# Scores of a differential attention: both softmax components as two 64-row matmuls under one exponential

## The chip, the cores and the metric

The kernel runs on the 8 cores of one Trainium2 chip, each core taking 2 of the 16 sequences; the cores exchange nothing. The metric is device time in microseconds (us) of the slowest core. Each core has a matmul engine (PE, TensorE), a vector engine (DVE), an activation engine (ACT), a general engine (POOL) and a queue that starts transfers (SP). They run side by side, each works its own instructions strictly in the order in which they stand, and they wait for each other on semaphores.

## The reference

One block: a normalised input is projected to five parts of 512 columns (a recurrent branch, its gate, q, k, v); a gated linear recurrence and a differential attention fill 1024 mixed columns; an output projection, then a gated feed-forward part of width 3072 with a short convolution, each with a residual; a last norm. The attention is the part that matters here:

```python
    q = q.reshape(bsz, s, DIFF_HEADS, 2, DIFF_QK)      # 4 heads, 2 components, 64 wide
    k = k.reshape(bsz, s, DIFF_HEADS, 2, DIFF_QK)
    v = v.reshape(bsz, s, DIFF_HEADS, DIFF_VDIM)       # 128 wide
    ...
        logits = jnp.einsum("bqhcd,bkhcd->bhcqk", qb, k).astype(jnp.float32) * scale   # 64 ** -0.5
        logits = logits + jnp.transpose(bias, (2, 0, 1))[None, :, None]   # same bias for both components
        mask = (k_pos // CHUNK)[None, :] <= (q_pos // CHUNK)[:, None]
        p = jax.nn.softmax(logits, axis=-1)
        w = p[:, :, 0] - lam * p[:, :, 1]
        return jnp.einsum("bhqk,bkhe->bqhe", w.astype(v.dtype), v)
```

So each head has two score matrices with a contraction of 64 each, one bias for both, two softmaxes, and one value product of their weighted difference.

## The kernel before

A core works on 8 groups of 512 positions (4 groups to a sequence). Everything is kept with channels on the 128 partitions and positions along the row. Dense work is a list of units, each of which fills one of three PSUM banks: 8 matmuls of 128x512 for a projection or feed-forward unit (lines 718, 726, 734), 24 for a unit of the feed-forward's way down (line 742). Weights come through a ring of three 1 MB slabs in SBUF. A unit's result is read out by ACT or DVE, after which the bank is free.

The attention of a group runs beside the dense units of the group before it. For each head and each block of 128 keys, and for each of the two components, there is one *tile*: a score matmul (line 1004) of 128 keys by up to 512 queries, on the diagonal and just beside it a bias addition by DVE in PSUM (line 1023), an exponential by ACT from PSUM to the bf16 tile `PT` (line 1026), and up to four matmuls of 128x129 with the values (line 1038), which gather the sum of the weights in their last column. There are 640 such tiles. The scores alternate between PSUM banks 0 and 1 (a pool "S" of two); the value sums stand in banks 2 to 4; dense units use 5 to 7.

A key tile `KT` holds a head's 128 rows: 64 of component 0 above 64 of component 1. The score matmul of one component uses all 128 rows. So that the other component adds nothing, the queries are kept twice in `qz`, each time with zeros in the other half's rows. `fin_q` (lines 748 to 766) writes them from PSUM with one instruction of 64 rows for each component, and POOL zeroes `qz` once at the start (line 494).

The order of the instructions is worked out when the program is built. `Flow.run` keeps a clock for each engine with an estimated duration for each operation (`t_pe`, `t_act`, `t_dve`, `t_pool`), and takes, again and again, the operation that could start first; ties go by priority, with attention tiles first. `attention` has a pace that spreads its tiles over the dense units. A tile gets a slot of "S" before its score matmul and gives it back once its exponential is placed. What comes out is one fixed list for each engine. Where an engine's real work is later than the estimate, the engines that wait for it wait in place.

Of the kernel before, what the change touches and what calls it, by code (L numbers as in the profile page):

```python
# [16 lines left out]
G = 512  # L17
# [360 lines left out]
def build(nseq, S, pk_off, npar, st_off, nst):  # L378
# [14 lines left out]
    with ExitStack() as st:  # L393
# [9 lines left out]
        qz = T("qz", [128, 4, 2, G], BF16)  # L403
# [4 lines left out]
        PT = T("PT", [128, 3, G], BF16)  # L408
# [12 lines left out]
        banks = [st.enter_context(nc.psum_tensor("pb%d" % i, [128, 512], F32)) for i in range(8)]  # L421
# [55 lines left out]
        SB = (0, 1)  # L477
# [16 lines left out]
        op("pool", lambda e: e.memset(qz[:], 0.0), writes=b_q, dur=4.0)  # L494
# [253 lines left out]
        def fin_q(g, h, bk):  # L748
            bank = DB[bk]
            if g > 0:  # L750
                yield need(("tq", g - 1, h))
            flip[0] ^= 1
            use_act = flip[0]
            for c in range(2):
                lo, hi = c * 64, c * 64 + 64
                if use_act:
                    yield o_act(G, lambda e, c=c, lo=lo, hi=hi: e.activation(out=qz[lo:hi, h, c, :],
                                                                            in_=banks[bank][lo:hi, :], func=AF.Copy,
                                                                            scale=0.125), [b_ps[bank]], [b_q[h]])
                else:  # L760
                    yield o_dve(G, lambda e, c=c, lo=lo, hi=hi: e.tensor_scalar(out=qz[lo:hi, h, c, :],
                                                                               in0=banks[bank][lo:hi, :],
                                                                               scalar1=0.125, scalar2=None,
                                                                               op0=ALU.mult), [b_ps[bank]], [b_q[h]])
            yield put("bank", bk)
            yield mark(("q", g, h))
# [218 lines left out]
        def attention(g, pace):  # L985
            qt = g % NG
            nj = qt * 4 + 4
            base = (g // NG) * NG
            tiles = [(h, j, c) for h in range(4) for j in range(nj) for c in range(2)]
            yield need(("setup",))  # L990
            for h in range(4):
                yield need(("q", g, h))
                yield need(("k", g, h))
                yield need(("v", g, h))
            for n, (h, j, c) in enumerate(tiles):
                if pace is not None:
                    yield need(("d", pace(n / len(tiles))))
                s_ = yield get("S")
                bank = SB[s_]
                i0 = max(0, j - qt * 4)  # L1000
                N = (4 - i0) * 128
                slot = (base + j // 4) % KVS
                jj = j % 4
                yield o_pe(t_pe(N), lambda e, bank=bank, N=N, slot=slot, h=h, jj=jj, c=c, i0=i0: e.matmul(  # L1004
                    banks[bank][:, 0:N], lhsT=KT[:, slot, h, jj * 128:(jj + 1) * 128], rhs=qz[:, h, c, i0 * 128:G],
                    start=True, stop=True), [b_K[slot][h], b_q[h]], [b_ps[bank]])
                if j == nj - 1 and c == 1:
                    yield mark(("tq", g, h))
                yield go(tile(g, n, h, j, c, s_, i0, N, slot, nj, n == len(tiles) - 1), P_T)

        def tile(g, n, h, j, c, s_, i0, N, slot, nj, last_tile):
            qt = g % NG
            bank = SB[s_]
# [7 lines left out]
            if wn:  # L1021
                bias_ap = pv("biasT", h * 256 + boff, h * 256 + boff + wn)
                yield o_dve(wn, lambda e: e.tensor_tensor(out=banks[bank][:, 0:wn], in0=banks[bank][:, 0:wn],  # L1023
                                                          in1=bias_ap, op=ALU.add), [b_ps[bank], b_bias], [b_ps[bank]])
            p = yield get("PT")
            yield o_act(N, lambda e: e.activation(out=PT[:, p, 0:N], in_=banks[bank][:, 0:N], func=AF.Exp),  # L1026
                        [b_ps[bank]], [b_PT[p]], "exp")
# [3 lines left out]
            if j == 0 and c == 0 and (g, h) != (0, 0):  # L1031
                yield need(("acc", g - 1, 3) if h == 0 else ("acc", g, h - 1))

            def f(e):
                for il in range(i0, 4):
                    ab, off = (AC + c, il * 130) if il < 3 else (AC + 2, c * 130)
                    st_flag = j == 0 and (il == 0 or (il == 3 and c == 0))
                    last = e.matmul(banks[ab][:, off:off + 129], lhsT=PT[:, p, (il - i0) * 128:(il - i0 + 1) * 128],  # L1038
                                    rhs=Va[:, slot * 4 + j % 4, h, 0:129], start=st_flag, stop=(j == qt * 4 + il),
                                    skip_group_check=True)  # L1040
                return last
            wb = [b_ps[AC + c], b_ps[AC + 2]] if i0 < 3 else [b_ps[AC + 2]]
            yield o_pe(t_pe(129, 4 - i0), f, [b_PT[p], b_V[slot][j % 4]], wb)
            yield put("PT", p)
            yield mark(("pv", g, n))
            if j == nj - 1 and c == 1:
# [245 lines left out]
        fl = Flow(S_, {"bank": 3, "S": 2, "PT": 3, "ring": NRING, "x": 8, "lru": 2, "ob": 1, "st": 2, **NPOOL})  # L1292
# [68 lines left out]
```

How the kernel before makes its waits and increments, by code:

```python
            def body(e):  # L149
                for fn, waits, sem, inc in self.prog[k]:
                    for s, v in waits:
                        e.wait_ge(self.sems[s], v)
                    if fn is not None:
                        ins = fn(e)
                        ins.then_inc(self.sems[sem], inc)
```

## Time and profile before

| | |
|---|---|
| median of 3 runs | 1935.11 us (1935.06 to 1939.55) |
| the profiled execution | 1935.9 us, span of its slowest core 1934.3 us |
| spans of the 8 cores | 1915.1 to 1934.3 us |
| PE busy | 1727.8 us, 89% of the span, 9458 matmuls |
| PE weight loads | 837.0 us |
| DVE, ACT, POOL busy | 1126.3, 1074.1, 583.7 us |

A "span" is the time from the first to the last instruction of a core. Of PE's busy time it has to be known that a matmul's record is longer than the distance between two of them: a 128x512 matmul has a record of 0.38 us, while 24 of them back to back take 5.34 us. What one costs in a stream is the distance. Idle time is counted before the instruction that ended it, with the engine and line that released it.

### The profile page before, as it was taken

How to read it: one execution, taken by the hardware profiler on the slowest of the kernel's cores; microseconds unless marked ns; L12 is line 12 of the kernel's file. 1: busy time of each engine (PE TensorE's matmuls, PEld its weight loads, DVE VectorE, ACT ScalarE, POOL GpSimd, SP SyncE). 2: the span in 40 equal slices, each digit the busy share in tenths (PEclk: the TensorE clock that was granted, in tenths of full speed). 3: DMA queues.
4: the chain of work that ended last, by engine and by line, in shares of the span. 5: the costliest groups of instructions: out<-in, count | busy, mean ns of one | idle time of the engine just before them, and what ended most of it. 6: DMA issues, size and time to landing. Idle time of an engine off the chain costs nothing.

```text
span 1934.3 us, 32122 instructions; the slowest of 8 cores (1915.1 to 1934.3 us)
## 1 busy us (share of the span) xinstructions
PE 1727.8 (89%) x9458; PEld 837.0 (43%) x9458; DVE 1126.3 (58%) x2136; ACT 1074.1 (56%) x1876; POOL 583.7 (30%) x809
## 2 busy tenths in 40 slices
PE   4774799599999989999999989999999998997996
PEld 1332344244444544444444444444444554543442
DVE  6753688327773367635884388625784167623741
ACT  3463577137782478833782277625785467932631
POOL 3523455332521214303440336112530212212201
PEclk9986899799999999999999999999999999998998
DMA  8998688434434326244634453433524334342542
GB/s 266 234 184 214 201 279 280 135 130 158 147 132 168 115 88 196 105 152 138 217 121 163 148 168 142 170 126 124 197 106 158 126 115 137 115 169 98 175 135 104
DMA packets 54569, 306.44 MB, mean 158 GB/s; under 512 B 5760, under 2 KB 5888, under 8 KB 30720
## 3 DMA queue, kind: packets, MB, share of 16 engines
q1 hardware_dynamic: 51200, 298.10, 46.6%
q0 software_dynamic: 3200, 6.29, 2.6%
q8 instruction: 81, 1.33, 0.3%
q14 instruction: 88, 0.72, 0.1%
HBM read 273.96 MB, written 42.99 MB: 164 GB/s over the span
## 4 chain that ended last, share of the span: by engine, by line
PE 80%; issue 5%; DVE 5%; ACT 5%; DMA 3%; POOL 1%; SPq 0%; DVEq 0%; ACTq 0%; POOLq 0%
PE pb L718 40%; PE pb L742 17%; PE pb L734 6%; PE pb L1004 5%; PE pb L1038 5%; PE pb L726 2%; PE pb L1253 2%; DMA xp<-wa 2%; ACT aT L815 1%; PE pb L562 1%; DMA tL<-x 1%; ACT PT L1026 1%; DVE H L603 1%; POOL tN L594 1%; DVE ob L1080 1%
## 5 line engine op out<-in xcount | busy, mean ns | idle before, releaser
L718 PE MATMUL pb<-H,ring 128*128 128x512 bf16 x3784 | 883.4, 385 | 53.5 <-ACT tL L834 22.6
L718 PEld LDWEIGHTS pb<-H,ring 128*128 128x128 bf16 x3784 | 362.6, 99 | 479.0 <-issue 104.3
L1026 ACT ACTIVATE PT<-pb 128x512 bf16<-128x512 f32 (+3 forms) x640 | 316.4, 533 | 312.0 <-PE pb L1004 195.7
L594 POOL TENSOR_TENSOR tN<-tN 128x512 f32<-128x512 f32 x161 | 206.3, 1282 | 543.0 <-ACT tN L583 537.9
L742 PE MATMUL pb<-aT,ring 128*128 128x512 bf16 x1536 | 340.5, 379 | 0.9 <-DVE aT L940 0.9
L953 DVE TENSOR_TENSOR xp<-pb,xp 128x512 f32<-128x512 f32 x128 | 88.4, 691 | 352.3 <-PE pb L742 234.7
L742 PEld LDWEIGHTS pb<-aT,ring 128*128 128x128 bf16 x1536 | 148.9, 98 | 177.8 <-issue 5.4
L1004 PE MATMUL pb<-qz,KT 128*128 128x512 bf16 (+3 forms) x640 | 190.8, 349 | 28.8 <-ACT PT L1026 26.1
L1038 PE MATMUL pb<-Va,PT 128*128 128x129 bf16 x2176 | 191.2, 221 | 26.8 <-DVE tO L1074 22.0
L940 DVE TENSOR_TENSOR aT<-pb,aT 128x512 bf16<-128x512 f32 x192 | 131.0, 685 | 119.3 <-PE pb L718 102.4
L1038 PEld LDWEIGHTS pb<-Va,PT 128*128 128x128 bf16 x2176 | 153.4, 98 | 99.1 <-issue 34.0
L583 ACT ACTIVATE tN<-xp 128x512 f32<-128x512 f32 x144 | 90.2, 630 | 189.4 <-DVE xp L953 173.8
L930 DVE SCALAR_TENSOR_TENSOR tG<-tG,prm 128x512 f32<-128x512 f32 x192 | 149.9, 786 | 52.5 <-ACT tG L923 51.2
L930 DVE SCALAR_TENSOR_TENSOR aT<-tG,prm 128x512 bf16<-128x512 f32 x192 | 159.4, 834 | 11.1 <-DVE tG L930 0.6
L923 ACT ACTIVATE tG<-pb,prm 128x512 f32<-128x512 f32 x192 | 150.3, 790 | 3.5 <-DVE aT L930 3.2
L919 ACT ACTIVATE tG<-pb 128x512 f32<-128x512 f32 x192 | 116.2, 606 | 64.0 <-PE pb L1253 33.6
L926 POOL COPY fhalo<-tG 128x2 f32<-128x2 f32 x192 | 68.0, 355 | 264.5 <-ACT tG L919 252.4
L1023 DVE TENSOR_TENSOR pb<-pb,prm 128x256 f32<-128x256 f32 (+1 forms) x304 | 106.8, 376 | 61.9 <-PE pb L1004 57.3
L734 PE MATMUL pb<-mixT,ring 128*128 128x512 bf16 x512 | 122.7, 388 | 1.9 <-ACT mixT L1104 1.9
L877 ACT ACTIVATE tL<-tL 128x512 f32<-128x512 f32 x192 | 111.9, 634 | 0.7
L1004 PEld LDWEIGHTS pb<-qz,KT 128*128 128x128 bf16 x640 | 62.7, 98 | 109.9 <-issue 45.2
L603 DVE SCALAR_TENSOR_TENSOR H<-xp,prm,tN 128x512 bf16<-128x512 f32 x120 | 85.5, 774 | 40.1 <-ACT tN L575 39.2
(95 smaller groups left out, 1518.4 us busy)
## 6 DMA issues: line engine op xcount, KB each, us to landing
ring<-wa SPq DMA_DIRECT2D x128, 1024.0 KB, 4.9
ring<-wd SPq DMA_DIRECT2D x64, 768.0 KB, 4.2
xp<-wa SPq DMA_DIRECT2D x38, 1024.0 KB, 8.5
xp<-x SPq DMA_DIRECT2D x64, 512.0 KB, 8.6
wa<-ring SPq DMA_DIRECT2D x17, 1024.0 KB, 11.2
out<-xp SPq DMA_DIRECT2D x32, 512.0 KB, 6.0
wd<-wd POOLq DMA_DIRECT2D x8, 768.0 KB, 80.6
tL<-x SPq DMA_DIRECT2D x4, 512.0 KB, 18.6
```

The costliest lines, as they stand in the source:

```text
L594: yield o_(G, lambda e: e.tensor_tensor(out=tN[:, acc, :], in0=tN[:, acc, :], in1=tN[:, sq, :], op=ALU.add), [b_N[acc], b_N[sq]], [b_N[acc]])
L718: last = e.matmul(banks[bank][:], lhsT=rv(r)[:, kk * 512 + c * 128:kk * 512 + (c + 1) * 128], rhs=hd[0][:, kk, :], start=(kk == 0), stop=( ...
L734: last = e.matmul(banks[bank][:], lhsT=rv(r)[:, kk * 512 + c * 128:kk * 512 + (c + 1) * 128], rhs=mixT[:, kk, :], start=(kk == 0), stop=(k ...
L742: last = e.matmul(banks[bank][:], lhsT=rv(r)[:, kk * 128:(kk + 1) * 128], rhs=aT[:, kk, :], start=(kk == 0), stop=(kk == 23))
L877: return o_act(G, lambda e: e.activation(out=tL[:, dst, 0:G], in_=tL[:, src, 0:G], func=func, **kw), [b_L[src]] + extra, [b_L[dst]], "exp")
L919: yield o_act(G, lambda e: e.activation(out=tG[:, gb, 2:514], in_=banks[bank][:], func=AF.Copy), [b_ps[bank]], [b_G[gb]])
L923: yield o_act(G, lambda e: e.activation(out=tG[:, ga, 0:G], in_=banks[bank][:], func=AF.Identity, scale=w(2), bias=pv("fcb", fc, fc + 1)), ...
L930: yield o_dve(G, lambda e, j=j, dst=dst: e.scalar_tensor_tensor(out=dst, in0=tG[:, gb, j:j + G], scalar=w(j), in1=tG[:, ga, 0:G], op0=ALU. ...
L940: yield o_dve(G, lambda e: e.tensor_tensor(out=aT[:, fc, :], in0=banks[bank][:], in1=aT[:, fc, :], op=ALU.mult), [b_ps[bank], b_aT[fc]], [ ...
L1004: yield o_pe(t_pe(N), lambda e, bank=bank, N=N, slot=slot, h=h, jj=jj, c=c, i0=i0: e.matmul(banks[bank][:, 0:N], lhsT=KT[:, slot, h, jj * ...
L1026: yield o_act(N, lambda e: e.activation(out=PT[:, p, 0:N], in_=banks[bank][:, 0:N], func=AF.Exp), [b_ps[bank]], [b_PT[p]], "exp")
L1038: last = e.matmul(banks[ab][:, off:off + 129], lhsT=PT[:, p, (il - i0) * 128:(il - i0 + 1) * 128], rhs=Va[:, slot * 4 + j % 4, h, 0:129], ...
```

## The change

Both components of a head and key block become one tile, so that there are 320 instead of 640. Its two score matmuls take 64 rows each: component 0 the upper half of the array (partitions 0 to 63 of `KT` and of the queries), component 1 the lower half (64 to 127), each into a bank of its own of one two-bank PSUM tensor `SP`. One DVE instruction adds the bias to both, one ACT instruction takes the exponential of both (up to 1024 columns), and up to eight value matmuls follow. The queries are kept once, without zeros, in `qT`, and are written by one instruction of 128 rows that `copy_op` gives to ACT and DVE in turn. The zeroing of `qz` goes. The pool "S" now has one slot, the pair of banks; it had two, one bank each. `PT` keeps three slots, each now for both components. The planner's estimate for the two score matmuls together is 1.3 times that of one.

```diff
-        qz = T("qz", [128, 4, 2, G], BF16)
+        qT = T("qT", [128, 4, G], BF16)
-        PT = T("PT", [128, 3, G], BF16)
+        PT = T("PT", [128, 3, 2, G], BF16)
-        banks = [st.enter_context(nc.psum_tensor("pb%d" % i, [128, 512], F32)) for i in range(8)]
+        SP = st.enter_context(nc.psum_tensor("SP", [128, 2, 512], F32))
+        banks = [None, None] + [st.enter_context(nc.psum_tensor("pb%d" % i, [128, 512], F32)) for i in range(2, 8)]
-        op("pool", lambda e: e.memset(qz[:], 0.0), writes=b_q, dur=4.0)
@@ fin_q
-            flip[0] ^= 1
-            use_act = flip[0]
-            for c in range(2):
-                ...
+            yield copy_op(qT[:, h, :], banks[bank][:], [b_ps[bank]], [b_q[h]], G, 0.125)
@@ attention
-            tiles = [(h, j, c) for h in range(4) for j in range(nj) for c in range(2)]
+            tiles = [(h, j) for h in range(4) for j in range(nj)]
-                yield o_pe(t_pe(N), lambda e, bank=bank, N=N, slot=slot, h=h, jj=jj, c=c, i0=i0: e.matmul(
-                    banks[bank][:, 0:N], lhsT=KT[:, slot, h, jj * 128:(jj + 1) * 128], rhs=qz[:, h, c, i0 * 128:G],
-                    start=True, stop=True), [b_K[slot][h], b_q[h]], [b_ps[bank]])
+                def f(e, N=N, slot=slot, h=h, jj=jj, i0=i0):
+                    for c in range(2):
+                        last = e.matmul(SP[:, c, 0:N], lhsT=KT[c * 64:c * 64 + 64, slot, h, jj * 128:(jj + 1) * 128],
+                                        rhs=qT[c * 64:c * 64 + 64, h, i0 * 128:G], start=True, stop=True)
+                    return last
+                yield o_pe(1.3 * t_pe(N), f, [b_K[slot][h], b_q[h]], [b_ps[0]])
@@ tile
-                yield o_dve(wn, lambda e: e.tensor_tensor(out=banks[bank][:, 0:wn], in0=banks[bank][:, 0:wn],
-                                                          in1=bias_ap, op=ALU.add), [b_ps[bank], b_bias], [b_ps[bank]])
+                yield o_dve(2 * wn, lambda e: e.tensor_tensor(
+                    out=SP[:, :, 0:wn], in0=SP[:, :, 0:wn], in1=bias_ap.unsqueeze(1).to_broadcast([128, 2, wn]),
+                    op=ALU.add), [b_ps[0], b_bias], [b_ps[0]])
-            yield o_act(N, lambda e: e.activation(out=PT[:, p, 0:N], in_=banks[bank][:, 0:N], func=AF.Exp),
-                        [b_ps[bank]], [b_PT[p]], "exp")
+            yield o_act(2 * N, lambda e: e.activation(out=PT[:, p, :, 0:N], in_=SP[:, :, 0:N], func=AF.Exp),
+                        [b_ps[0]], [b_PT[p]], "exp")
             def f(e):
-                for il in range(i0, 4):
-                    ...
+                for c in range(2):
+                    for il in range(i0, 4):
+                        ...
-            yield o_pe(t_pe(129, 4 - i0), f, [b_PT[p], b_V[slot][j % 4]], wb)
+            yield o_pe(t_pe(129, 2 * (4 - i0)), f, [b_PT[p], b_V[slot][j % 4]], wb)
-        fl = Flow(S_, {"bank": 3, "S": 2, "PT": 3, "ring": NRING, "x": 8, "lru": 2, "ob": 1, "st": 2, **NPOOL})
+        fl = Flow(S_, {"bank": 3, "S": 1, "PT": 3, "ring": NRING, "x": 8, "lru": 2, "ob": 1, "st": 2, **NPOOL})
```

In the changed program the lines have other numbers: the score matmul is line 993, the value matmuls are line 1029, the dense ones 717, 725, 733 and 741.

The change moves the instructions on every engine, since the planner starts from other durations and slots. PE before, where the down units (line 742) begin beside the attention of a later group; `qz` are the queries with zeros, `KT` the keys, `Va` the values, `PT` the exponentials, `aT` the feed-forward's activations:

```order
L742 MATMUL pb<-aT,ring 128x512 x24
L1004 MATMUL pb<-qz,KT 128x512 x2
L742 MATMUL pb<-aT,ring 128x512 x24
L1004 MATMUL pb<-qz,KT 128x512 x2
L1038 MATMUL pb<-Va,PT 128x129 x8
L742 MATMUL pb<-aT,ring 128x512 x24
```

And PE in the changed program at the same place:

```order
L741 MATMUL pb<-aT,ring 128x512 x24
L993 MATMUL SP<-qT,KT 128x512 x2
L741 MATMUL pb<-aT,ring 128x512 x24
L993 MATMUL SP<-qT,KT 128x512 x2
L1029 MATMUL pb<-Va,PT 128x129 x8
L741 MATMUL pb<-aT,ring 128x512 x24
```

Here the two lists stand alike; only the two score matmuls are now a pair on the two halves, with 128-row work ahead of and behind it. In the whole program the score matmuls stood in 425 runs on PE, cut by other work, and now stand in 313.

The second place is the end of the last group's attention, behind the last dense unit that is left to put between. PE before:

```order
L1004 MATMUL pb<-qz,KT 128x512
L1038 MATMUL pb<-Va,PT 128x129 x4
L1004 MATMUL pb<-qz,KT 128x512
L1038 MATMUL pb<-Va,PT 128x129 x4
L1004 MATMUL pb<-qz,KT 128x384
L1038 MATMUL pb<-Va,PT 128x129 x4
L1004 MATMUL pb<-qz,KT 128x384
L1038 MATMUL pb<-Va,PT 128x129 x4
L1004 MATMUL pb<-qz,KT 128x256
L1038 MATMUL pb<-Va,PT 128x129 x3
```

And PE in the changed program there:

```order
L993 MATMUL SP<-qT,KT 128x512 x2
L1029 MATMUL pb<-Va,PT 128x129 x8
L993 MATMUL SP<-qT,KT 128x512 x2
L1029 MATMUL pb<-Va,PT 128x129 x8
L993 MATMUL SP<-qT,KT 128x384 x2
L1029 MATMUL pb<-Va,PT 128x129 x8
L993 MATMUL SP<-qT,KT 128x256 x2
L1029 MATMUL pb<-Va,PT 128x129 x6
L993 MATMUL SP<-qT,KT 128x128 x2
```

Before, a score matmul could run into one bank while the exponential read the other. Now each pair of score matmuls stands behind the exponential of the pair before it, with eight value matmuls between. Over the whole program, of the 319 distances from one key block's first score matmul to the next one's, 22 had fewer than 4 matmuls of 512 columns of other work in them before, and 25 have now; 122 now have about one 8-matmul unit.

## Rows read from the trace of the kernel before

**Rows 1.** The page: busy time, share of span, instructions; then the clock.
```profile
PE 1727.8 (89%) x9458; PEld 837.0 (43%) x9458; DVE 1126.3 (58%) x2136; ACT 1074.1 (56%) x1876; POOL 583.7 (30%) x809
...
PEclk9986899799999999999999999999999999998998
```
**Rows 2.** The page: the chain that ended last, by engine.
```profile
PE 80%; issue 5%; DVE 5%; ACT 5%; DMA 3%; POOL 1%; SPq 0%; DVEq 0%; ACTq 0%; POOLq 0%
```
**Rows 3.** Three stretches: length; busy us of PE, PEld, DVE, ACT, POOL; clock; DMA.
```profile
0.00:400.00 400.00, 282.04 (x1442) 130.48 (x1443) 246.77 (x461) 198.57 (x362) 165.51 (x176) 0.88 0.80 222
400.00:1700.00 1300.00, 1246.28 (x7046) 614.91 (x7045) 786.51 (x1525) 795.88 (x1395) 375.97 (x565) 0.99 0.42 143
1700.00:1934.30 234.30, 199.44 (x972) 91.58 (x970) 93.06 (x150) 79.67 (x119) 42.25 (x70) 0.94 0.40 133
```
**Rows 4.** The middle stretch, line 1004 alone: PE, PEld.
```profile
400.00:1700.00 1300.00, 152.20 (x512) 50.03 (x512) 0.99 0.42 143
```
**Rows 5.** Waits of PE in 400 to 1700: us in total, times, longest.
```profile
PE pb L718 <- ACT tL L834: 19.8, 6, 4.9
PE pb L1004 <- ACT PT L1026: 12.8, 14, 2.8
PE pb L718 <- ACT tG L923: 4.8, 7, 1.1
```
**Rows 6.** Timeline from 612 us: start, duration, engine, line.
```profile
612.20 0.59 PE L1004 MATMUL pb<-qz,KT 128*128 128x512 bf16 x2
...
612.63 0.62 PE L1038 MATMUL pb<-Va,PT 128*128 128x129 bf16 x8
612.68 1.10 ACT L1026 ACTIVATE PT<-pb 128x512 bf16<-128x512 f32 x2 [4.01 <-PE pb L1004]
...
613.09 5.34 PE L742 MATMUL pb<-aT,ring 128*128 128x512 bf16 x24
```
**Rows 7.** Groups by form, PE and its weight loads: busy, mean ns, idle before.
```profile
L742 PE MATMUL pb<-aT,ring 128*128 128x512 bf16 x1536 | 340.5, 379 | 0.9 <-DVE aT L940 0.9
L1004 PE MATMUL pb<-qz,KT 128*128 128x512 bf16 x448 | 145.7, 381 | 16.1 <-ACT PT L1026 14.1 <-DVE ob L1088 0.8 <-DVE pb L1023 0.2
...
L1004 PEld LDWEIGHTS pb<-qz,KT 128*128 128x128 bf16 x640 | 62.7, 98 | 109.9 <-issue 45.2
```
**Rows 8.** Groups by form, exponentials, bias additions and the writing of the queries.
```profile
L1026 ACT ACTIVATE PT<-pb 128x512 bf16<-128x512 f32 x448 | 250.0, 598 | 235.1 <-PE pb L1004 195.7 <-PE pb L1038 20.8 <-DVE pb L1023 13.1
L1026 ACT ACTIVATE PT<-pb 128x128 bf16<-128x128 f32 x64 | 16.8, 277 | 26.5 <-DVE pb L1023 23.7 <-DVE sm L1055 1.9 <-PE pb L1038 0.3
L757 ACT ACTIVATE qz<-pb 64x512 bf16<-64x512 f32 x34 | 20.1, 591 | 37.9 <-PE pb L718 32.9 <-PE pb L1038 2.4 <-PE pb L1004 1.2
...
L1023 DVE TENSOR_TENSOR pb<-pb,prm 128x256 f32<-128x256 f32 x192 | 77.1, 426 | 37.9 <-PE pb L1004 37.4
L1023 DVE TENSOR_TENSOR pb<-pb,prm 128x128 f32<-128x128 f32 x112 | 31.3, 292 | 24.0 <-PE pb L1004 19.9 <-PE pb L1038 3.4
L761 DVE TENSOR_SCALAR qz<-pb 64x512 bf16<-64x512 f32 x30 | 20.6, 686 | 17.3 <-PE pb L718 14.7 <-PE pb L1004 1.7
```
**Rows 9.** Timeline from 1736 us, in the last group's attention.
```profile
1736.43 0.38 PE L1004 MATMUL pb<-qz,KT 128*128 128x512 bf16 x1 [0.34 <-ACT PT L1026]
1736.92 0.43 DVE L1023 TENSOR_TENSOR pb<-pb,prm 128x256 f32<-128x256 f32 x1 [0.65 <-PE pb L1004]
1737.56 0.60 ACT L1026 ACTIVATE PT<-pb 128x512 bf16<-128x512 f32 x1 [0.48 <-DVE pb L1023]
1738.30 0.32 PE L1004 MATMUL pb<-qz,KT 128*128 128x384 bf16 x1 [0.47 <-ACT PT L1026]
...
1740.00 0.27 PE L1004 MATMUL pb<-qz,KT 128*128 128x256 bf16 x1 [0.37 <-ACT PT L1026]
```
**Rows 10.** POOL at the start: the zeroing, then the first cast of weights.
```profile
L494 POOL MEMSET qz<- 128x4096 bf16 x1 | 3.5, 3511 | 0.0
...
16.17 1.89 POOL L1191 CAST ring<-xp 128x2048 bf16<-128x2048 f32 x1 [11.22 <-DMA xp<-wa]
```

**Rows 11.** Waits over the whole span, the one for the slot of the scores.
```profile
PE pb L1004 <- ACT PT L1026: 26.1, 29, 3.2
```

More of the change, by code:

```diff
@@ L476, in build @@
         DB = (5, 6, 7)
-        SB = (0, 1)
         AC = 2
@@ L751, in fin_q @@
                 yield need(("tq", g - 1, h))
-            flip[0] ^= 1
-            use_act = flip[0]
-            for c in range(2):
[L755 to L764, printed above, removed]
+            yield copy_op(qT[:, h, :], banks[bank][:], [b_ps[bank]], [b_q[h]], G, 0.125)
             yield put("bank", bk)
@@ L994, in attention @@
                 yield need(("v", g, h))
-            for n, (h, j, c) in enumerate(tiles):
+            for n, (h, j) in enumerate(tiles):
                 if pace is not None:
@@ L998, in attention @@
                 s_ = yield get("S")
-                bank = SB[s_]
                 i0 = max(0, j - qt * 4)
@@ L1003, in attention, with tile @@
                 jj = j % 4
-                yield o_pe(t_pe(N), lambda e, bank=bank, N=N, slot=slot, h=h, jj=jj, c=c, i0=i0: e.matmul(
-                    banks[bank][:, 0:N], lhsT=KT[:, slot, h, jj * 128:(jj + 1) * 128], rhs=qz[:, h, c, i0 * 128:G],
-                    start=True, stop=True), [b_K[slot][h], b_q[h]], [b_ps[bank]])
-                if j == nj - 1 and c == 1:
+                def f(e, N=N, slot=slot, h=h, jj=jj, i0=i0):
[4 more added lines that the diff above has]
+                yield o_pe(1.3 * t_pe(N), f, [b_K[slot][h], b_q[h]], [b_ps[0]])
+                if j == nj - 1:
                     yield mark(("tq", g, h))
-                yield go(tile(g, n, h, j, c, s_, i0, N, slot, nj, n == len(tiles) - 1), P_T)
-        def tile(g, n, h, j, c, s_, i0, N, slot, nj, last_tile):
+                yield go(tile(g, n, h, j, s_, i0, N, slot, nj), P_T)
+        def tile(g, n, h, j, s_, i0, N, slot, nj):
             qt = g % NG
-            bank = SB[s_]
             d0 = qt * 4 + i0 - j
@@ L1030, in tile @@
                 yield need(("pv", g, n - 1))
-            if j == 0 and c == 0 and (g, h) != (0, 0):
+            if j == 0 and (g, h) != (0, 0):
                 yield need(("acc", g - 1, 3) if h == 0 else ("acc", g, h - 1))
             def f(e):
-                for il in range(i0, 4):
[L1036 to L1040, printed above, removed]
-                return last
-            wb = [b_ps[AC + c], b_ps[AC + 2]] if i0 < 3 else [b_ps[AC + 2]]
-            yield o_pe(t_pe(129, 4 - i0), f, [b_PT[p], b_V[slot][j % 4]], wb)
+                for c in range(2):
+                    for il in range(i0, 4):
+                        ab, off = (AC + c, il * 130) if il < 3 else (AC + 2, c * 130)
+                        st_flag = j == 0 and (il == 0 or (il == 3 and c == 0))
+                        last = e.matmul(banks[ab][:, off:off + 129],
+                                        lhsT=PT[:, p, c, (il - i0) * 128:(il - i0 + 1) * 128],
+                                        rhs=Va[:, slot * 4 + j % 4, h, 0:129], start=st_flag, stop=(j == qt * 4 + il),
+                                        skip_group_check=True)
+                return last
+            wb = [b_ps[AC], b_ps[AC + 1], b_ps[AC + 2]] if i0 < 3 else [b_ps[AC + 2]]
+            yield o_pe(t_pe(129, 2 * (4 - i0)), f, [b_PT[p], b_V[slot][j % 4]], wb)
             yield put("PT", p)
             yield mark(("pv", g, n))
-            if j == nj - 1 and c == 1:
+            if j == nj - 1:
                 yield mark(("tpv", g, h))
```

## The prediction, on record before the changed kernel ran

> **What bounds the kernel now.** I read the busy shares first [rows 1]: PE 89%, the next engine 58%. The reader is to see that PE is the only candidate for the whole, and that its clock stands near full. Next the chain that ended last [rows 2], of which 80% is PE. Then stretches [rows 3], since a share is an average: from 400 to 1700 us PE is busy 1246 of 1300 us at clock 0.99, while in the first 400 us, with DMA at 0.80, it is busy 282, and in the last 234 us it is busy 199. The waits in the middle stretch [rows 5] are small: 12.8 us for the exponential's slot, 19.8 for a read-out by ACT, 4.8 for another. So from 400 to 1700 us what counts is how long PE's stream is. 512 of the 640 score matmuls lie there [rows 4]; a microsecond taken from them there is nearly a microsecond of the span.
>
> What a score matmul costs is read from a distance, not from its record. At 612.20 us two of them start, and the value matmuls behind them start at 612.63, 0.43 us later; 24 dense matmuls take 5.34 us with a last record of 0.38, so 0.2157 each [rows 6, 7]. Its column time therefore is 0.2157 us for 512 columns, 0.162, 0.108 and 0.054 for 384, 256 and 128. The zeros cost as much as anything else.
>
> **The change part by part.** (a) *The two halves abreast.* 448 of 640 tiles have 512 columns [rows 7], and 64 each have 384, 256 and 128. As pairs: 224 x 0.2157 + 32 x (0.162 + 0.108 + 0.054) = 48.3 + 10.4 = 58.7 us of stream go if the second half runs entirely beside the first. The 0.8 of them in the middle stretch count in full, the rest by half, since PE is idle 118 of 400 and 35 of 234 us there: 0.9 x 58.7 = 52.8 us. Nothing else in the program uses part of the array, so the trace does not show that two halves run abreast. Its bounds are 58.7 us and nothing.
>
> (b) *The change of the array's shape.* The score matmuls stand in 313 runs between 128-row work, so the array goes over to halves and back 313 times. The trace has no such change. From below: nothing, since different 128-row matmuls follow each other without a gap (0.43 us for two, [rows 6]). From above: the new work starts only when the last matmul has left the array and its weights are then loaded. A record is 0.379 and the distance 0.2157 us [rows 7], so 0.163 us hang over; the weight load is 0.098 us. That is 0.261 a change, 0.52 for both, 313 x 0.52 = 163 us. Between such ends I take one uncovered weight load per pair, 0.098 us, the nearest row for what a load can't hide if the array in front of it is of another shape: 313 x 0.098 = 30.7, and 0.9 of it is 27.6 us. The point at which (a) and (b) cancel is 0.188 us per pair.
>
> The Trainium skill, on the page TensorEngine Tiling, section Overview and its Key Properties under Tiling Modes, says that a change of tiling mode, unlike a change of tile, needs TensorE to be drained. It speaks against this change. No row here shows it. If it holds in full, the sum is that of the second rival below.
>
> The page TensorE: Matmul & The Clock Gate, Part 3, says that matmuls on different row groups start about 4 ns apart, and that a weight load overlaps matmuls in flight when it is for another row group. By that (a) would be within 320 x 0.004 = 1.3 us of the full 58.7, by estimate. No row here shows it either.
>
> (c) *ACT and DVE get shorter.* An exponential takes 598 ns for 512 columns and 277 for 128 [rows 8], 0.84 ns a column and 170 ns besides. One of 1024 columns is then 1.03 us instead of 1.20, and 320 fixed parts of 0.17 go: 54 us of ACT's 1074. The bias addition: 426 ns for 256 columns, 292 for 128, 1.05 ns a column and 158 besides; 152 of these go, 24 us of DVE. The queries: 34 and 30 instructions of 64 rows at 591 and 686 ns [rows 8] become 32 of 128 rows, whose length goes by columns, so about 0.6 and 0.7 each: 20 us over both engines, and a bank is free some 0.6 us earlier. Most of it lies beside PE. What counts are PE's waits for ACT, 19.8 + 12.8 + 4.8 in the middle [rows 5]: I give a fifth of these 37, so 7 us. Bounds: 0 and 25.
>
> (d) *The zeroing.* 3.5 us of POOL [rows 10] go, but POOL then sits 11.2 us until the weights' DMA lands. Worth nothing; were the DMA earlier, 3.5.
>
> (e) *One slot instead of two.* This is the wait that the change adds: the next pair's score matmul waits for the exponential of the pair before, and all of PE is queued behind it. The loop without bias: 0.48 from the score matmul's start to the exponential (612.20 to 612.68, [rows 6]), 1.03, and 0.14 back to PE (an exponential ends at 1737.56 + 0.60, the score matmul starts at 1738.30, [rows 9]): 1.65 us. With bias 0.49 + (0.69 + 0.21) + 1.03 + 0.14 = 2.56. Where a dense unit of 8 stands between, PE has 8 x 0.216 + 8 value matmuls in 0.46 + the pair 0.22 = 2.41 us of work, which covers the loop without bias by 0.76 and nearly the one with it. Beside a down unit (5.2 us) it is covered threefold. Not covered are the 25 distances without dense work. In the last group's attention a key block now takes 1738.30 to 1740.00 = 1.70 us [rows 9], and would take 2.56 with bias: five such blocks, 4 us. For the 18 others 0.3 each, since 22 stood so before, 5 us. Sum +9; bounds 0 and 40 (the second is a rival).
>
> *The sum:* -52.8 + 27.6 - 7 + 9 = -23 us. The profiled execution has 1934.3 us of span in 1935.9 us of time, and the median of the runs is 1935.1, the same within a microsecond; so 1912 us for the median.
>
> **The rivals.** *1. The halves come free.* No cost for (b): 1912 - 28 = 1884 us. For it speaks that today's weight loads are wholly under the matmuls; against it that they are of one shape.
>
> *2. The array empties at each change* (slower). Place: the matmul ahead of each run of score matmuls and the one behind it. Price: the 0.163 us overhang twice, 313 x 0.326 = 102 us, 0.9 of it 92, instead of the 27.6 of (b): 1912 - 28 + 92 = 1976 us. With both weight loads uncovered too, 163 x 0.9 = 147, and 2031. It decides from 0.188 us per pair on. For it: a record's overhang is real time before a result is there, and a partial sum of 128 rows has to pass the rows that the halves take over. Against it: PE streams over all changes of operand, bank and type without any idle time.
>
> *3. The single slot holds PE.* Place: the 122 distances with about one unit. An exponential of 1.03 us queued behind ACT's 0.6 and 0.8 us read-outs is late by as much; if half of the 0.76 us margin is exceeded by 0.5 us at each biased or delayed one, 122 x 0.3 = 37 us: 1949 us. For it: PE waits for this slot already with two of them. Against: the planner's order puts a pair where it finds ACT free, and its loop was covered.
>
> *4. The halves run one after the other.* (a) and (b) fall away together: 1912 + 53 - 28 = 1937 us. For it: two weight loads stand between two matmuls in the order of the program. Against: nothing in the trace.
>
> **How the numbers follow.** Chances: my forecast 0.38, rival 1 0.15, rival 2 0.29, rival 3 0.09, rival 4 0.09. About 0.3%, 6 us, can be told from no change here. The forecast's own spread (1895 to 1930; b from 0.05 to 0.15 us a pair) gives faster 0.32, same 0.04, slower 0.02; rival 1 faster 0.15; rival 2 same 0.01, slower 0.28; rival 3 same 0.02, slower 0.07; rival 4 faster 0.02, same 0.05, slower 0.02. Sum: faster 0.49, same 0.12, slower 0.39. The range reaches below rival 1 by 10 us for more of (c), 1874, and above rival 2 by 12 us, 1988, and leaves out its dearer form. The forecast's own range is 1895 to 1930.
>
> **What would show it.** (a): the second score matmul's record starts well under 0.2 us after the first. (b): the distance from the end of dense streaming to the first score matmul, and from the pair to the value matmuls: pair and both changes together below 0.43 us if I am right (0.31 by the forecast), above it if rival 2 holds. (c): exponentials of 1.03 us, bias additions of 0.69. (e): PE's waits for the exponential's slot, 26 us over the span before [rows 11], at most 40 now; rival 3 would show some 60 or more. Wrong in kind I would be if the clock fell in the middle stretch, or if PE's waits for read-outs by ACT grew.

## The result: slower by 1.85%

The changed kernel takes 1969.82, 1970.83, 1971.04 and 1979.10 us, against a median of 1936.28 us for the kernel before beside it: a ratio of 1.0185, 95% interval 1.0155 to 1.0216. (Two more executions, of 2053 and 2084 us, in which the cores of one die had a clock of 0.89 to 0.91, are left out, as are such executions of every kernel below.) I had forecast 1912, a gain of 23 us; it lost 36 by the ratio and 34 between the two profiled executions, from which the accounts below are made.

The page of the profiled execution: busy time of each engine, and the chain that ended last.

```profile
span 1968.3 us, 30379 instructions; the slowest of 8 cores (1952.8 to 1968.3 us)
PE 1737.7 (88%) x9458; PEld 789.4 (40%) x9458; DVE 1103.2 (56%) x1969; ACT 1036.0 (53%) x1539; POOL 579.7 (29%) x808
...
PE 75%; DMA 6%; ACT 6%; issue 5%; DVE 5%; POOL 2%; SPq 0%; DVEq 0%; ACTq 0%; POOLq 0%
```

PE is busy 10 us longer than before [rows 1], in a span that is 34 us longer, although 59 us of columns are gone from its stream. ACT lost 38 us of work and DVE 23, and neither bought anything. The middle stretch, in the columns of [rows 3]:

```profile
400.00:1700.00 1300.00, 1219.43 (x6865) 559.68 (x6864) 750.53 (x1358) 740.21 (x1090) 362.71 (x557) 0.98 0.41 140
```

In the same 1300 us PE gets through 6865 matmuls instead of 7046, with 27 us more idle. Two things have to be found: why the stream did not get shorter, and where the idle time comes from.

**The stream.** The timeline of the changed kernel around 606 us, beside [rows 6]; PEld are weight loads, and "issue" means that the trace shows nothing that they waited for:

```profile
601.11 5.35 PE L741 MATMUL pb<-aT,ring 128*128 128x512 bf16 x24
...
606.39 0.10 PEld L993 LDWEIGHTS SP<-qT,KT 64*128 64x128 bf16 x2 [0.42 <-issue]
606.39 0.39 PE L993 MATMUL SP<-qT,KT 64*128 64x512 bf16 x2
...
606.71 0.45 PEld L1029 LDWEIGHTS pb<-Va,PT 128*128 128x128 bf16 x8 [0.23 <-issue]
606.72 0.63 PE L1029 MATMUL pb<-Va,PT 128*128 128x129 bf16 x8
606.88 1.02 ACT L1016 ACTIVATE PT<-SP 128x1024 bf16<-128x1024 f32 x1 [4.07 <-PE SP L993]
607.18 5.34 PE L741 MATMUL pb<-aT,ring 128*128 128x512 bf16 x24
...
612.46 0.39 PE L993 MATMUL SP<-qT,KT 64*128 64x512 bf16 x2
```

The two halves do run abreast: both matmuls lie in 0.39 us, the record of one. From start to start they are 0.003 us apart. But 24 dense matmuls start at 601.11 and the pair at 606.39, 5.28 us later, where 24 x 0.2157 is 5.18: 0.10 us more. And the value matmuls start 0.33 us after the pair, not 0.22. The two losses together are nearly as long as the matmul that was saved. From one pair to the next it is 612.46 - 606.39 = 6.07 us. In the kernel before, value matmuls and 24 dense ones with two whole-array score matmuls take 6.07 us as well: the two that start at 612.20 [rows 6] have their successors at 618.27:

```profile
618.27 0.59 PE L1004 MATMUL pb<-qz,KT 128*128 128x512 bf16 x2
```

The weight loads show how. Before, the load for the next matmul starts 0.002 us after the current one, under its columns. Where a pair follows a dense matmul it starts only 0.307 us after that one (on the way out 0.315), so 0.091 us behind its columns, with its own matmul within 0.005 us of it. The median distance from a dense matmul to a pair is 0.312 us instead of 0.216, and from a 512-column pair to a value matmul 0.319 instead of 0.216. It does not depend on how long the matmul ahead is: behind a value matmul (0.056 us) the shortest distance to a pair is 0.152. So 0.096 us on the way in, 0.103 on the way out, at any length.

This is what the Trainium skill's page TensorEngine Tiling says in its Key Properties: changing the mode drains the engine, changing the tile does not. The trace agrees that there is a price, and puts it at 0.10 us a change. That is less than the 0.163 us by which a record outlasts its distance [rows 7], so the wait is not for all of that overhang. What the engine waits for in that time no row tells. And the 4 ns between starts on different row groups, from the Trainium skill's page TensorE: Matmul & The Clock Gate, Part 3, are 3 ns here.

**The whole account.** I added up the distances from the start of each matmul to the start of the next, on each core, and divided each into columns at full clock, changes of shape, what runs at half clock (the extra time of matmuls that take twice their distance), and waits. Medians of the six cores whose records are complete, in us:

| kernel | columns | changes | half clock | waits | core's span |
|---|---|---|---|---|---|
| before | 1663.0 | 0 | 30.5 | 197.6 | 1921.8 |
| changed | 1604.2 | 62.3 | 38.2 | 223.3 | 1965.5 |
| difference | -58.8 | +62.3 | +7.7 | +25.7 | +43.7 |

(4 us more are small distances of the half matmuls over their columns. The median spans lie 43.7 us apart, the slowest cores' 34, so these terms come to somewhat more than the loss in time.) The halves come out at +3.5 to +8 us; the rest is waits and the slow clock behind them. Who waits, over the whole span of the slowest core, us in total, times, longest:

```profile
PE SP L993 <- ACT PT L1016: 32.3, 28, 3.9
PE pb L733 <- POOL mixT L892: 29.2, 4, 9.8
PE pb L561 <- POOL tN L593: 22.3, 3, 10.1
```

The wait for the score slot is 32 us against 26 [rows 11]. The second is new: the output projection waits for the last of the recurrences, in four places. The timeline at 1091 us shows one, and what it costs beyond the wait:

```profile
1091.04 0.38 PE L851 MATMUL pb<-xcb,bdw 128*128 128x512 bf16 x1
...
1099.78 1.16 POOL L892 TENSOR_TENSOR mixT<-gg,tL 128x512 bf16<-128x512 bf16 x1 [3.52 <-DVE tL L881]
...
1101.19 3.57 PE L733 MATMUL pb<-mixT,ring 128*128 128x512 bf16 x8 [9.77 <-POOL mixT L892]
```

The recurrence's gate matmul (line 851) stands in PE's list only at 1091 us, with the whole chain of ACT, DVE and POOL still to come. PE stands 9.8 us. The granted clock is 1.00 before 1091 us, falls to 0.50 (1.2 GHz) at 1094.6, 3 us into the stall, and comes back at 1104.9; the 8 matmuls at 1101.19 take 3.57 us instead of 1.89.

### The profile page after: what moved, and what is told of

The parts are those of the page before. It is cut to its first block, busy times and chain, and to the rows that moved or that the text cites. A ratio compares the mean times of both kernels' runs of the same rounds, so it can differ in the third digit from the quotient of the medians.

```text
span 1968.3 us, 30379 instructions; the slowest of 8 cores (1952.8 to 1968.3 us)
## 1 busy us (share of the span) xinstructions
PE 1737.7 (88%) x9458; PEld 789.4 (40%) x9458; DVE 1103.2 (56%) x1969; ACT 1036.0 (53%) x1539; POOL 579.7 (29%) x808
## 3 DMA queue, kind: packets, MB, share of 16 engines
q1 hardware_dynamic: 51200, 298.10, 45.1%
## 4 chain that ended last, share of the span: by engine, by line
PE 75%; DMA 6%; ACT 6%; issue 5%; DVE 5%; POOL 2%; SPq 0%; DVEq 0%; ACTq 0%; POOLq 0%
PE pb L717 37%; PE pb L741 16%; PE pb L1029 6%; PE pb L733 6%; PE SP L993 4%; DMA xp<-wa 4%; PE pb L1245 2%; PE pb L725 2%; DMA wa<-aT 2%; ACT PT L1016 1%; ACT tL L864 1%; DVE H L602 1%; PE pb L561 1%; ACT aT L802 1%; POOL ring L1183 1%
## 5 line engine op out<-in xcount | busy, mean ns | idle before, releaser
L1016 ACT ACTIVATE PT<-SP 128x1024 bf16<-128x1024 f32 (+1 forms) x320 | 286.7, 896 | 321.0 <-PE SP L993 199.5
L1029 PE MATMUL pb<-Va,PT 128*128 128x129 bf16 x2176 | 177.4, 224 | 10.9 <-DVE tO L1066 6.8
L1029 PEld LDWEIGHTS pb<-Va,PT 128*128 128x128 bf16 x2176 | 130.0, 99 | 72.2 <-issue 56.7
L917 DVE SCALAR_TENSOR_TENSOR aT<-tG,prm 128x512 bf16<-128x512 f32 x192 | 152.6, 799 | 9.4 <-DVE tG L917 0.2
L906 ACT ACTIVATE tG<-pb 128x512 f32<-128x512 f32 x192 | 115.3, 604 | 75.4 <-PE pb L1245 38.2
L733 PE MATMUL pb<-mixT,ring 128*128 128x512 bf16 x512 | 127.8, 402 | 30.2 <-POOL mixT L892 29.2
L913 POOL COPY fhalo<-tG 128x2 f32<-128x2 f32 x192 | 72.5, 378 | 272.5 <-ACT tG L906 264.3
L993 PE MATMUL SP<-qT,KT 64*128 64x512 bf16 (+3 forms) x640 | 115.8, 357 | 39.1 <-ACT PT L1016 32.3
L1012 DVE TENSOR_TENSOR SP<-SP,prm 128x512 f32<-128x512 f32 (+1 forms) x152 | 90.5, 595 | 82.9 <-PE SP L993 82.3
L993 PEld LDWEIGHTS SP<-qT,KT 64*128 64x128 bf16 x640 | 31.8, 93 | 170.4 <-issue 169.9
```

The costliest lines, as they stand in the source:

```text
L733: last = e.matmul(banks[bank][:], lhsT=rv(r)[:, kk * 512 + c * 128:kk * 512 + (c + 1) * 128], rhs=mixT[:, kk, :], start=(kk == 0), stop=(k ...
L906: yield o_act(G, lambda e: e.activation(out=tG[:, gb, 2:514], in_=banks[bank][:], func=AF.Copy), [b_ps[bank]], [b_G[gb]])
L917: yield o_dve(G, lambda e, j=j, dst=dst: e.scalar_tensor_tensor(out=dst, in0=tG[:, gb, j:j + G], scalar=w(j), in1=tG[:, ga, 0:G], op0=ALU. ...
L993: last = e.matmul(SP[:, c, 0:N], lhsT=KT[c * 64:c * 64 + 64, slot, h, jj * 128:(jj + 1) * 128], rhs=qT[c * 64:c * 64 + 64, h, i0 * 128:G], ...
L1016: yield o_act(2 * N, lambda e: e.activation(out=PT[:, p, :, 0:N], in_=SP[:, :, 0:N], func=AF.Exp), [b_ps[0]], [b_PT[p]], "exp")
L1029: last = e.matmul(banks[ab][:, off:off + 129], lhsT=PT[:, p, c, (il - i0) * 128:(il - i0 + 1) * 128], rhs=Va[:, slot * 4 + j % 4, h, 0:129 ...
```

## Experiments

Each ratio is to the kernel before on the same chip, with its 95% interval in brackets. Experiments 5, 6 and 7 rest on one time each and have no interval. Theory A, formed from the trace above: the changes of shape eat the halves' gain, and the rest lies in the order of the instructions, with the single slot. Rival B: work on half the array slows the kernel in another way too. Rival C: the single slot is the loss.

**1. The same order on the whole array.**

```diff
-  matmul(SP[:, c, 0:N], lhsT=KT[c * 64:c * 64 + 64, slot, h, ...], rhs=qT[c * 64:c * 64 + 64, h, i0 * 128:G])
+  matmul(SP[:, c, 0:N], lhsT=KT[:, slot, h, ...], rhs=qT[:, h, i0 * 128:G])
```

> The changed kernel, instruction for instruction in the same order on every engine, but each score matmul takes all 128 rows of the keys and of the queries (so both banks get the sum of the two components: that part of the result is left out). No change of the array's shape is left, and no two halves run abreast. Theory A (a run of half-array matmuls costs about 0.10 us on the way in and 0.10 on the way out, 313 runs, 62 us, against 59 us of stream saved; the remaining loss is in the planner's new order): the stream grows by 59, 62 go, so the time stays within 10 us of the changed kernel, near 1966. Rival B (half-array work itself is what slows the kernel, by the clock or by longer matmuls around it): it falls back to some 1935 to 1945. Rival C (single slot holds PE): also about 1966, so this run tells only A or C from B.

Measured: 1.0239 (1.0197 to 1.0282), lowest run 1974.89 us. Columns 1663.0, changes 0, waits 227.6, half clock 40.9. B falls: without a single half-array matmul, and with the same list on every engine, the kernel is as slow as the changed one. (The lowest time lies 9 us above the 1966 expected, at the edge of the 10 allowed; the two intervals overlap.) The timeline at the place above, with the 6.07 us again (608.87 - 602.80):

```profile
602.80 0.59 PE L993 MATMUL SP<-qT,KT 128*128 128x512 bf16 x2
603.23 0.62 PE L1029 MATMUL pb<-Va,PT 128*128 128x129 bf16 x8
603.69 5.34 PE L741 MATMUL pb<-aT,ring 128*128 128x512 bf16 x24
608.87 0.59 PE L993 MATMUL SP<-qT,KT 128*128 128x512 bf16 x2
```

**2. The halves alone**, in the kernel before: `qT` without zeros, everything else (two slots, one exponential and one bias each) as it was.

```diff
-  matmul(banks[bank][:, 0:N], lhsT=KT[:, slot, h, ...], rhs=qz[:, h, c, i0 * 128:G])
+  matmul(banks[bank][:, 0:N], lhsT=KT[c * 64:c * 64 + 64, slot, h, ...], rhs=qT[c * 64:c * 64 + 64, h, i0 * 128:G])
```

> The kernel before, with its two score slots, one exponential and one bias addition for each component, but queries kept once and each score matmul on its half of the array. Theory A: 425 runs of score matmuls on PE at 0.2 us are 85 us, and the 215 places where two stand side by side save 43 us of stream: +42, about 1977. Rival C (the single slot is the loss, changes of shape are cheap): 1935 - 43 + little, 1895 to 1935. Rival B: slower with a lower clock outside of waits.

Measured: 1.0196 (1.0174 to 1.0218), lowest run 1970.27 us. 424 runs of half-array matmuls are 84.4 us of changes, and the columns fall by 38.7, not 43. The two terms come to +46, with +42 forecast and 38 by the ratio. With two slots the halves lose outright, since more score matmuls stand alone: 424 runs against 313 are 35% more changes, and 35% more of their cost.

**3. One exponential and one slot alone**, on the whole array with zeros. The exponentials' tile `PT` has two slots here instead of three, since a third does not fit beside the zeros.

```diff
-  matmul(SP[:, c, 0:N], lhsT=KT[c * 64:c * 64 + 64, ...], rhs=qT[c * 64:c * 64 + 64, h, i0 * 128:G])
-  yield o_pe(1.3 * t_pe(N), f, ...)          # "S": 1, "PT": 3
+  matmul(SP[:, c, 0:N], lhsT=KT[:, ...], rhs=qz[:, h, c, i0 * 128:G])
+  yield o_pe(2 * t_pe(N), f, ...)            # "S": 1, "PT": 2
```

> The changed kernel's single slot, one exponential and one bias addition for both components, but full-array score matmuls against queries with zeros as before (planner's estimate 2 matmuls; two exponential tiles instead of three, since a third does not fit beside the zeros). No change of shape is left. Theory A: stream as before; what differs from 1936 is the planner's order and shorter ACT and DVE work: 1920 to 1955. Rival C (the slot holds PE): 1960 or more, with PE waits for the exponential of over 50 us.

Measured: 1.0112 (1.0091 to 1.0134), lowest 1955.71 us, just above what A gave (1955) and below what C gave (1960). PE's waits for the exponential are 24 us, not over 50, so C as I had put it (the slot's own wait) fails. Yet the waits altogether are 211.1 us and half clock 45.1, 28 us over the kernel before. (How much of them is the missing third slot of `PT`, no run tells.)

**4. The planner told the price.**

```diff
-  yield o_pe(1.3 * t_pe(N), f, ...)
+  yield o_pe(t_pe(N) + 0.2, f, ...)
```

> The changed kernel with the planner's estimate for the two score matmuls set to what the trace shows, one matmul and 0.2 us, instead of 1.3 matmuls. PE's work is the same. If the extra waits (29 us on the mixed columns before the output projection) come from an order that was planned on too small a number, it gains 15 to 30 us: 1940 to 1955. If the waits are chance of a greedy order, the time moves by up to 20 us either way. If the planned number has no part in it, 1970.

Measured: 1.0064 (1.0046 to 1.0082), lowest 1945.61 us: 22 us better than the changed kernel, with waits of 198.9. The waits for the mixed columns fell from 29.2 to 6.2 us. That looked like proof that the wrong estimate was to blame; experiments 8 and 9 say otherwise.

**5. The recurrence earlier.**

```diff
-  yield go(lru(g, c, xc), P_BG if g else P_SMALL)
+  yield go(lru(g, c, xc), P_SMALL)
```

> The changed kernel, but the recurrence's chains have the priority of small work in every group instead of background. In the changed kernel PE stands 29 us, in four places, before an output projection that waits for the last recurrence (POOL's product into the mixed columns); in the kernel before it waits for that nowhere for long. If these places are a matter of which chain gets a bank late, the waits for the mixed columns fall below 10 us here. Whether the whole gets shorter is open, since the recurrence then delays read-outs: 1950 to 1990.

Measured: 1987.03 us. The wait for the mixed columns fell as expected:

```profile
PE pb L733 <- POOL mixT L892: 4.6, 1, 4.6
```

The waits as a whole did not: 224.7 us, and half clock 56.4. A stall taken away by hand came back elsewhere (PE's wait for a read-out of line 910 went from 11 to 21.7 us).

**6. The kernel before with one slot**: `"S": 1` in place of `"S": 2`.

> The kernel before with one score slot instead of two, all else as it was: 640 tiles through a single bank. Each tile's loop (0.48 from the score matmul to the exponential, 0.60, 0.14 back) is 1.22 us, 1.76 with a bias, and 640 of them have to find cover. If a single slot is what costs time, this is far slower, 1980 or more. If one slot is as good as two, 1935 to 1950.

Measured: 2187.83 us. The wait for the slot, and the clock with it:

```profile
PE pb L1004 <- ACT PT L1026: 168.9, 209, 3.2
...
PEclk9767997999987999569999999999987999856998
```

So one slot is not as good as two: with 640 tiles through it the waits are 378.6 us and half clock 94.5. Putting both components under one exponential takes most of that back.

**7. Half of the keys as weights.** Both banks are cleared once, since the partitions of the other 64 keys are not written any more, and the bias goes to 64 partitions. The order of PE, ACT, DVE and POOL is that of the changed kernel, but for the clearing.

```diff
-  matmul(SP[:, c, 0:N], lhsT=KT[..., jj * 128:(jj + 1) * 128], ...)
+  matmul(SP[0:64, c, 0:N], lhsT=KT[..., jj * 128:jj * 128 + 64], ...)
```

> The changed kernel, order as it is, but each score matmul takes only 64 of the 128 keys of its block as its stationary operand (the other 64 keys' scores are left out). It asks what the 0.096 us before a pair are. If they are the weight load that can't be done ahead, the distance from the last whole-array matmul to the pair falls from 0.311 us to about 0.26; if they are a fixed price of the change of shape it stays at 0.31. The way out, 0.103 us, has whole weights in both cases and should stay. Whole time 1950 to 1975.

Measured: 1981.48 us, above the 1950 to 1975 expected.

```profile
611.92 5.35 PE L742 MATMUL pb<-aT,ring 128*128 128x512 bf16 x23
...
617.20 0.11 PEld L994 LDWEIGHTS SP<-qT,KT 64*64 64x64 bf16 x2 [0.42 <-issue]
617.21 0.40 PE L994 MATMUL SP<-qT,KT 64*64 64x512 bf16 x2
...
617.54 0.45 PEld L1030 LDWEIGHTS pb<-Va,PT 128*128 128x128 bf16 x8 [0.23 <-issue]
...
L994 PEld LDWEIGHTS SP<-qT,KT 64*64 64x64 bf16 x640 | 35.2, 104 | 171.6 <-issue 171.1
```

and in the changed kernel:

```profile
L993 PEld LDWEIGHTS SP<-qT,KT 64*128 64x128 bf16 x640 | 31.8, 93 | 170.4 <-issue 169.9
```

The median distance from a dense matmul to the pair is 0.309 us, not 0.26. So the number of weight columns does not set it. But this does not show that it is no weight load: the 0.26 took for granted that 64 columns load in half the time, and the load's record is 104 ns for them, against 93 for 128. Against the load speaks only that its record is 11 ns longer here while the distance is 3 ns shorter. (The dense group shows 23 of its 24 matmuls, one record is missing. The shape is now 64 by 64, and the way out rises to 0.333 - 0.216 = 0.117.)

**8 and 9. Other numbers for the planner.** The estimate for a pair set to `t_pe(N) + 0.15`, and to `1.2 * t_pe(N)`; nothing else.

> The changed kernel with the planner's estimate for a pair of score matmuls set to one matmul and 0.15 us (before: 1.3 matmuls, 1970; one matmul and 0.20: 1947). PE's own work is the same in all of them. If the 20 us between the last two came from telling the planner the truth, this lies between them, near 1955. If they are chance of a greedy order, any value from 1930 to 1970 can come, and 1947 is not a limit.

> The changed kernel with the estimate at 1.2 instead of 1.3 matmuls, farther from the truth. Truth theory: 1970 or more. Chance theory: 1930 to 1980, by the waits that happen to come; the sum of stream, changes of shape, waits and slow clock will tell which term moved.

Measured, in this order: 1.0026 (0.9992 to 1.0060), lowest 1937.19 us; and 1.0081 (1.0057 to 1.0105), lowest 1949.01 us. The truth theory falls on both: the number between gives the best order so far, and the number farthest from the truth beats the changed kernel by 20 us. The estimate did not have to be right, it had to be another one. (I had named the 1.2 as a help against the truth theory; that 1.3 to 1.2 is worth 1% was not foreseen in size.)

**10. The control: the kernel before with another number** (`1.1 * t_pe(N)`).

> The kernel before, with the planner's estimate for a score matmul 1.1 times as large. Nothing else is changed. It is the control for the chance of the order: if the kernel before moves as much as the changed one does (10 us and more), then of the 34 us lost by the change the part in waits and slow clock is no property of the change. If it stays within 5 us of 1935, the two-slot kernel is less sensitive, and the sensitivity belongs to the single slot.

Measured: 0.9966 (0.9946 to 0.9987), lowest 1923.64 us. It moves too, by 7 us, between my two cases.

**11. The kernel before with another number and pace** (`1.05 * t_pe(N)`, and `p1 - 6` for `p1 - 4` in the pace).

> The kernel before with the estimate 1.05 times as large and the attention's pace ending six dense units before the next queries instead of four. As a second control for the chance of the order, and as a try at a version that beats both kernels: 1915 to 1945. Theory A (the two-slot, whole-array kernel has 62 us of changes less and 59 of stream more) makes this no worse than the changed kernel with any order.

Measured: 0.9929 (0.9912 to 0.9946), median 1920.00 us of 4 runs. It beats both kernels. Its gain is in the order alone: waits 186.9 us and half clock 27.4, against 197.6 and 30.5.

```profile
span 1920.8 us, 32128 instructions; the slowest of 8 cores (1901.1 to 1920.8 us)
...
PE pb L1004 <- ACT PT L1026: 18.6, 16, 3.2
```

**12. The order of 8 on the whole array**, the edit of experiment 1.

> The kernel with the estimate of 0.15 us, again in exactly its order, but every score matmul on the whole array (both banks get the sum of the two components: that part of the result is left out). A second matched pair for the price of the halves, in an order with few waits. Theory A: stream +59, changes of shape -63, so within 5 us of 1940. If the halves cost more than the sum of the two terms when PE is hardly waiting, it falls to 1925 or less.

Measured: 1.0032 (1.0017 to 1.0047), lowest 1938.36 us, against 1.0026 with halves. A second matched pair without a difference.

**13 and 14. The other pace with one slot**: on the whole array (edit 3, with `1.9 * t_pe(N)` and `p1 - 6`), and with halves (`t_pe(N) + 0.21` and `p1 - 6`).

> One exponential and one slot for both components on the whole array with zeros (the third experiment, 1956), with the planner's estimate 1.9 instead of 2 matmuls and the attention's pace ending six units before the next queries. If the 20 us that the third experiment lost belong to the single slot, it stays above 1945. If they are chance of the order, 1920 to 1940 can come, as for the kernel before in another order (1920).

> The changed kernel with an estimate of one matmul and 0.21 us and the same pace as above, ending six units before the next queries. The pace gave the kernel before 1920. If pace and order are worth the same here: 1925 to 1940, the lowest of this kernel's orders so far being 1940, and still not below 1920, since the halves save nothing net.

Measured: 1.0014 (0.9975 to 1.0053), lowest 1939.62 us; and 1.0043 (1.0026 to 1.0060), lowest 1942.47 us. Both near the kernel before, neither near 1920. 13 lies at the upper edge of the range for chance and under that for the slot, so it does not decide alone; 14 lies 2 us above its range. The orders together, medians over the cores as above, waits and half clock added:

| | ratio | waits + half clock |
|---|---|---|
| two slots, whole array: before, 10, 11 | 1, 0.9966, 0.9929 | 228, 224, 214 |
| one slot, whole array: 3, 13 | 1.0112, 1.0014 | 256, 232 |
| one slot, halves: changed, 4, 8, 9, 14 | 1.0185, 1.0064, 1.0026, 1.0081, 1.0043 | 262, 233, 230, 241, 229 |

The means are 222 us with two slots and 240 with one. The ranges meet: the best order with one slot has 229 us and the kernel before 228, and the ratios of 8 and 13 are not clear of 1. (Not in the table: experiments 1, 7 and 12, which have the order of another one; 2, with two slots and halves; and 5, one slot and halves, with 281 us. The whole-array kernels with one slot also have one slot of `PT` less.)

## Why the prediction was wrong

**(a) The halves abreast: right.** 58.7 us of columns were forecast, 58.8 are gone, and the second half starts 3 ns after the first.

**(b) The change of shape: a price per change, as forecast, but mis-sized by half.** "I take one uncovered weight load per pair, 0.098 us": it is about 0.10 us at each of the two changes, 0.199 per run of score matmuls, 62.3 us instead of 30.7. The point that I had named for break-even, 0.188 us per pair, lies just under it. The sign that I had named for it was too coarse to see this: a pair of 512 columns with both changes takes 0.216 + 0.199 = 0.415 us, under the 0.43, and the shorter pairs turn the sum. The row of the weight load had nearly the right size by accident, and was put in once. Experiments 1 and 12, each with the order of its partner, carry the sum of (a) and (b), and experiment 2 the size. What the price consists of stays open: experiment 7 shows only that it does not follow the number of weight columns. The second rival had the direction, but its price, the full overhang of 0.163 us at each change and 1976 us, is not what happened: it came near the measured 1970 through the wrong term.

**(c) Shorter ACT and DVE: the saving oversized, and worth next to nothing.** The exponential of 1024 columns takes 1.025 us (1.03 forecast), the bias addition 0.694 (0.69):

```profile
L1016 ACT ACTIVATE PT<-SP 128x1024 bf16<-128x1024 f32 x224 | 229.5, 1025 | 233.9 <-PE SP L993 199.5 <-DVE SP L1012 16.6 <-PE pb L1029 8.4
...
L1012 DVE TENSOR_TENSOR SP<-SP,prm 128x512 f32<-128x512 f32 x96 | 66.6, 694 | 66.1 <-PE SP L993 65.8
```

But "1.03 us instead of 1.20" misread [rows 6]: two exponentials back to back took 1.10 us there, not 1.20, since their records overlap. So the exponentials have 34 us less (320.6 to 286.6) and not 54, and ACT as a whole 38. DVE's bias additions have 18 less (108.4 to 90.5) and not 24. The queries' 20 us came as forecast. I gave 7 us for all of it. The three waits of [rows 5], 37.4 us, are 33.7 in the same stretch now, so some 4 us at most came of it. Of the two signs for being wrong in kind neither appeared clearly: the clock of the middle stretch went from 0.99 to 0.98, and the two waits for read-outs by ACT in [rows 5] fell from 24.6 to 17.3.

**(d) The zeroing:** no trace of it, as said.

**(e) One slot: the loop right, the effect missed.** In the last group the key blocks with bias are 1771.18 - 1768.61 = 2.57 us apart (2.56 forecast), and without 1.72 (1.65):

```profile
1764.64 0.39 PE L993 MATMUL SP<-qT,KT 64*128 64x512 bf16 x2 [0.76 <-ACT PT L1016]
...
1766.36 0.39 PE L993 MATMUL SP<-qT,KT 64*128 64x512 bf16 x2 [0.76 <-ACT PT L1016]
...
1768.61 0.39 PE L993 MATMUL SP<-qT,KT 64*128 64x512 bf16 x2 [1.30 <-ACT PT L1016]
...
1771.18 0.51 PE L993 MATMUL SP<-qT,KT 64*128 64x384 bf16 x2 [1.62 <-ACT PT L1016]
```

PE's waits for the exponential rose by 6 us, within the 9 that I gave. (The 18 other distances of this term should have been 25 - 5 = 20, which is 0.6 us.) But I looked for new waits only where PE waits for the slot, and took the rest of the order to cost what it had cost. The planner, with other tiles, slots and durations, finds another order for everything, and in this one PE waits 29 us for recurrences whose gate matmul stands late in its list, and then runs at half clock. The third rival's direction was right and its place wrong.

So two steps failed. Of the 57 us between forecast and result (34 + 23), 32 x 0.9 = 28 are (b), and the rest is waits and half clock, which I had counted at +9 - 7 and which grew by 25.7 + 7.7 = 33. With (b) at its measured size the forecast would have been 1912 + 28 = 1940, no clear change; the loss itself comes from the second step. Of the 33 us that these two grew, other orders of the same kernel give back 21 to 33 (experiments 4, 8, 9, 14): this part is an accident of the order. What stays with one slot in the best orders, 229 against 214 to 228, is small. Whether it is the slot's own price or too few orders tried is open: seven orders with one slot and three with two (experiments 2 and 5 aside) are not a distribution, and a kernel with two slots for pairs, which would need four banks, was not run.

## What to carry to other kernels

Half-array matmuls save their columns in full, but on this kernel each run of them amid whole-array work costs 0.2 us. A run has to save more than that: by these rows a single pair of 512 columns (0.216 us) breaks even and shorter ones lose. Runs of several pairs were not tried. Count the runs on the engine's own list before building it. And where a planner orders the work, compare two designs over several orders each: here one changed number in the planner, with no change of the work, moved the time by up to 1.6%, about as much as the change under study. The fastest kernel of this study (1920 us) came from two such numbers, the estimate and the pace, alone.

## What was not expected of the hardware

- The price of a change between the whole array and 64 rows hardly varies here: 0.096 us in, behind a matmul of 512 columns or of 129, and 0.103 out, behind 512, 384, 256 or 128 columns. With weights of 64 columns instead of 128 the way in is 0.309 us against 0.312 from start to start.
- A weight load of 64 rows by 64 columns is no shorter than one of 64 by 128: 104 ns against 93.
- The next weight load, which otherwise starts 0.002 us after the matmul ahead of it, starts 0.091 us after that one's columns are through where the shape changes.
- The stall of 9.8 us cost more than itself: the granted clock fell to 0.50 inside it, and the 8 matmuls behind it took 3.57 us instead of 1.89.
- Two exponentials of 512 columns back to back take 1.10 us, though the record of each is 0.598.
